# The two-layer loop written out on every engine, with constants where a register counted the layer

## What is computed

```python
for layer in range(DEPTH):                      # DEPTH = 2
    shift, scale, gate = ada_modulation(c, w_mod_mix[layer], b_mod_mix[layer])
    h = normalize(x) * (1.0 + scale) + shift
    mix = token_mixer(h, ...)                   # stick-breaking attention, pooling mixer,
                                                # sliding-window attention, sigmoid gates, w_out
    x = layer_norm(DEEPNORM_ALPHA * x + (1.0 + gate) * mix, ln_mix_g[layer], ln_mix_b[layer])
    shift, scale, gate = ada_modulation(c, w_mod_ffn[layer], b_mod_ffn[layer])
    h = normalize(x) * (1.0 + scale) + shift
    if layer % 2 == 0:
        ff = swiglu(h, ffn_w1[0], ffn_w3[0], ffn_w2[0])          # D_FF = 2816
    else:
        ff = moe_swiglu(h, w_router[0], b_router[0], exp_w1[0], exp_w3[0], exp_w2[0])
                                                # 8 experts of width 3584, the best 2 for each token
    x = layer_norm(DEEPNORM_ALPHA * x + (1.0 + gate) * ff, ln_ffn_g[layer], ln_ffn_b[layer])
```

## Time and profile before

| | before |
|---|---|
| median of 3 runs | 1914.64 us (1914.64, 1905.44, 1916.42) |
| span of the profiled execution | 1919.3 us |
| PE busy | 1731.4 us (90%) |
| DVE busy | 1421.4 us (74%) |
| ACT busy | 1042.3 us (54%) |
| POOL busy | 25.5 us (1%) |
| DMA | 503.98 MB, mean 263 GB/s |

### The profile page before, as it was taken

The page is one execution under the profiler, slowest core; times in us unless marked ns, Lnnn a source line. Parts: engine busy times, 40 slices in busy tenths (PEclk is TensorE's granted clock), DMA queues, the critical chain, the costliest instruction groups (busy, mean ns, idle before and its releaser), DMA issues.

```text
span 1919.3 us, 22270 instructions
## 1 busy us (share of the span) xinstructions
PE 1731.4 (90%) x7882; PEld 1390.2 (72%) x7883; DVE 1421.4 (74%) x1201; ACT 1042.3 (54%) x817; POOL 25.5 (1%) x31
## 2 busy tenths in 40 slices
PE   1899979996999949989979989999899899999995
PEld 0787758885877727868868868887687687787784
DVE  7776877757676776877868866656588688787787
ACT  1465434433555326757747745554577576675773
POOL 0100000000000000000000000000000000000000
PEclk9998989998999969999999999999999999999998
DMA  9874458754665436987978965666599699799892
GB/s 367 309 271 144 154 186 315 275 182 171 249 214 179 145 115 240 357 327 274 362 288 306 363 253 197 219 219 219 180 354 380 236 362 363 278 359 344 300 362 83
DMA packets 210686, 503.98 MB, mean 263 GB/s; under 512 B 9137, under 2 KB 13409, under 8 KB 210481
## 3 DMA queue, kind: packets, MB, share of 16 engines
q1 hardware_dynamic: 208770, 496.15, 72.3%
q0 software_dynamic: 1712, 5.43, 0.9%
HBM read 500.50 MB, written 1.05 MB: 261 GB/s over the span
## 4 chain that ended last, share of the span: by engine, by line
PE 79%; DVE 10%; issue 8%; ACT 2%; DMA 1%; DVEq 0%; ACTq 0%; SPq 0%
PE ps L1241 22%; PE ps L1243 22%; PE ps L1242 22%; DVE w_lo L772 2%; PE ps L1247 2%; PE ps L1248 2%; PE ps L1644 2%; PE ps L1530 2%; PE ps L1686 1%; DVE mod_acc L797 1%; ACT w_hi L457 1%; DVE stats L817 1%; PE ps L1365 1%; DVE gates L966 1%; PE ps L1366 1%
## 5 line engine op out<-in xcount | busy, mean ns | idle before, releaser
L772 DVE TENSOR_TENSOR w_lo<-w_raw,w_hi 128x2048 fp32r<-128x2048 f32 x423 | 966.4, 2291 | 381.7 <-ACT w_hi L457 381.1
L457 ACT CAST w_hi<-w_raw 128x2048 fp32r<-128x2048 f32 x423 | 806.5, 1910 | 352.0 <-PE ps L1243 282.7
L1241 PE MATMUL ps<-w_hi,actT_hi 128*128 128x512 f32 (+1 forms) x1536 | 613.8, 400 | 60.0 <-issue 40.2
L1243 PE MATMUL ps<-w_hi,actT_lo 128*128 128x512 f32 (+1 forms) x1536 | 600.0, 391 | 0.0
L1242 PE MATMUL ps<-w_lo,actT_hi 128*128 128x512 f32 (+1 forms) x1536 | 599.4, 390 | 0.0
L1241 PEld LDWEIGHTS ps<-w_hi,actT_hi 128*128 128x128 f32 x1536 | 294.3, 192 | 132.3 <-issue 60.9
L1243 PEld LDWEIGHTS ps<-w_hi,actT_lo 128*128 128x128 f32 x1536 | 293.3, 191 | 61.6
L1242 PEld LDWEIGHTS ps<-w_lo,actT_hi 128*128 128x128 f32 x1536 | 294.8, 192 | 57.5 <-issue 1.0
L1241 PE MATMUL ps<-w_hi,gT_hi 128*128 128x512 f32 x536 | 213.1, 398 | 16.3 <-DVE gT_lo L1058 14.1
L1243 PE MATMUL ps<-w_hi,gT_lo 128*128 128x512 f32 x536 | 213.6, 398 | 0.0
L1242 PE MATMUL ps<-w_lo,gT_hi 128*128 128x512 f32 x536 | 213.2, 398 | 0.0
(11 more groups left out here) (225 smaller groups left out, 1070.3 us busy)
## 6 DMA issues: line engine op xcount, KB each, us to landing
w_raw<-in_exp_w_dram SPq DMA_DIRECT2D x336, 1024.0 KB, 7.0
w_raw<-in_ffn_w_dram SPq DMA_DIRECT2D x33, 1024.0 KB, 5.2
w_raw<-in_w_mod_mix_dram SPq DMA_DIRECT2D x24, 1024.0 KB, 8.1
w_raw<-in_w_mod_ffn_dram SPq DMA_DIRECT2D x24, 1024.0 KB, 5.3
w_raw<-in_w_gate_dram SPq DMA_DIRECT2D x24, 1024.0 KB, 5.7
w_raw<-in_w_in_dram SPq DMA_DIRECT2D x14, 1024.0 KB, 7.3
w_raw<-in_w_out_dram SPq DMA_DIRECT2D x8, 1024.0 KB, 5.1
w_raw<-in_w_branch_c_dram SPq DMA_DIRECT2D x4, 1024.0 KB, 5.0
```

The source lines that it names most:

```text
L457: nc.scalar.copy(w_hi[:, j % SPLIT, :], w_raw[:, i % RING, :]).then_inc(split_hi, 1)
L772: TTn(w_lo[:, j % SPLIT, :], w_raw[:, i % RING, :], w_hi[:, j % SPLIT, :].bitcast(F32), ALU.subtract).then_inc(piece_used, 1)
L1241: MM(to, hi, w_h, start=first, stop=False)
L1243: return MM(to, lo, w_h, start=False, stop=last)
```

## The change

On all five engines the loop `Fori(0, DEPTH)` becomes Python's `for layer in range(DEPTH)`, so the code of the token mixer is laid down twice, once for each layer, and `layer` is a number when the program is built. `If(layer < 1)` / `Else` becomes Python's `if` / `else`, so the dense half stands behind the first mixer and the expert half behind the second, with no branch between. Waits that counted with a register have a constant. No arithmetic, no buffer, no transfer and no order of work on any engine is altered, and the experts' loop with its own branches stays.

```diff
--- before.py
+++ after.py
@@ -385,11 +385,11 @@
             stream(MOD0, 0, None, mod_layer=("mix", 0))
-            with sp.Fori(0, DEPTH) as layer:
+            for layer in range(DEPTH):
                 stream(MIX, layer * LAYER_PIECES + MOD0.n, layer, mod_layer=("ffn", layer), gap=layer * (RING // 2))
-                with sp.If(layer < 1):
+                if layer < 1:
                     stream(DENSE, MOD0.n + MIX.n, 0, mod_layer=("mix", 1), gap=RING // 2)
-                with sp.Else():
+                else:
                     moe0 = MOD0.n + LAYER_PIECES + MIX.n
                     sp.wait_ge(piece_used, moe0 + RING)
@@ -417,7 +417,7 @@
             gp.dma_start(cst[:, C_PAST:], consts[:, C_PAST:]).then_inc(tables_loaded, 16)
-            with gp.Fori(0, DEPTH) as layer:
+            for layer in range(DEPTH):
                 gp.wait_ge(gate1_ready, layer * 2 + 1)
                 gp.dma_start(sinks[:, :], I["sinks"][bass.ds(layer, 1), :].rearrange("a h -> (a h)").partition_broadcast(P)).then_inc(small_loaded, 16)
@@ -432,12 +432,12 @@
                         I["ln_mix_b"][bass.ds(layer, 1), :].rearrange("a d -> (a d)"))
-                with gp.If(layer < 1):
+                if layer < 1:
                     gp.wait_ge(gate_sent, 2)
                     fresh_acc(I["b_mod_mix"][1:2, :], 2)
                     gp.wait_ge(x_ready, 2)
                     ln_rows(I["ln_ffn_g"][0], I["ln_ffn_b"][0])
-                with gp.Else():
+                else:
                     gp.wait_ge(x_ready, 4)
                     nc.gpsimd.memset(yacc[:, :, :], 0.0).then_inc(yacc_zero, 1)
@@ -518,7 +518,7 @@
 
-            with act.Fori(0, DEPTH) as layer:
+            for layer in range(DEPTH):
                 sbase = layer * LAYER_SPLITS
                 chain = Chain(act, act_mix, layer * ACT_MIX_STEPS)
@@ -670,11 +670,11 @@
 
-                with act.If(layer < 1):
+                if layer < 1:
                     stream(DENSE, [MOD0.landed[s] + MIX.landed[s] for s in range(RING)], MIX.n_split,
                            panel_events(DENSE, DENSE_PANELS, MIX.n_split, 0, 2))
                     norms(2, 6, 4, 0, lambda i: round_piece(MIX, i, [layer_loads[s] + MOD0.landed[s] for s in range(RING)], LAYER_SPLITS))
-                with act.Else():
+                else:
                     act.wait_ge(rt_loaded, 32)
                     A(w_rt_hi[:, :, :], w_rt[:, :, :], ACT.Copy).then_inc(rt_hi, 1)
@@ -910,7 +910,7 @@
 
-            with dve.Fori(0, DEPTH) as layer:
+            for layer in range(DEPTH):
                 sbase = layer * LAYER_SPLITS
                 chain = Chain(dve, dve_mix, layer * DVE_MIX_STEPS)
@@ -1087,7 +1087,7 @@
 
-                with dve.If(layer < 1):
+                if layer < 1:
                     chain = Chain(dve, dve_ffn, 0)
                     stream(DENSE, [MOD0.landed[s] + MIX.landed[s] for s in range(RING)], MIX.n_split,
@@ -1095,7 +1095,7 @@
                     assert chain.n == DVE_DENSE_STEPS, chain.n
-                with dve.Else():
+                else:
                     chain = Chain(dve, dve_ffn, DVE_DENSE_STEPS)
                     step = chain.step
@@ -1290,7 +1290,7 @@
             open_sublayer(0, 4, 0, MOD0.n)
-            with pe.Fori(0, DEPTH) as layer:
+            for layer in range(DEPTH):
                 pbase = layer * LAYER_PIECES + MOD0.n
 
@@ -1605,11 +1605,11 @@
 
-                with pe.If(layer < 1):
+                if layer < 1:
                     swiglu(DENSE, DENSE_PANELS, MOD0.n + MIX.n, 0, 2)
                     pe.wait_ge(piece_used, LAYER_PIECES + MOD0.n + RING)
                     open_sublayer(2, 4, 0)
-                with pe.Else():
+                else:
                     second_tile(3, 4)
                     open_tile(3, 0, 1)
```

## The result

The changed kernel takes 1928.78 us (median of 6 runs, 1926.59 to 1933.76), the kernel before 1914.67 us (median of 6, 1905.44 to 1918.67). The ratio is 1.0088, with a 95% interval from 1.0065 to 1.0112. The forecast was 1906 us, with a range up to 1919 us: it was wrong in its sign and in its range.

A forecast was written before the change was run, and what follows sets the result against it. It took TensorE (PE), busy 90% of the span, as the bound, with its uncovered far jumps as the gain: 6.7 + 2.0 + 0 + 0 = 8.7 us off the 1914.64 us median, giving 1906 us, range 1896 to 1919 us.

The forecast's parts named there:

- Part 1: At the layer loop's closing, PE's bare jump back goes and the third weight piece starts earlier: 6.7 us gained.
- Part 2: Where the second layer branches to the experts, VectorE's jump goes and line 1102 follows line 858 directly: 2.0 us gained.
- Part 3: Register additions for the token mixer's waits run in the sequencers ahead of the engines: priced at 0, other end 1 us.
- The covered jumps: Jumps of ScalarE, GpSimd and SyncE in the layers, and PE's own to the experts, lie behind other work: 0.
- Part 4: In the experts' loop the code moves but keeps its size: priced at 0, with both ends put into rivals.
- Rival 2: Experts' code lies worse; two cheap boundaries turn dear, or each round pays one more fetch: 1914.7 us, chance 0.18.
- Rival 1: Experts' code lies better and PE keeps the body from the first rounds on: 1893 us, chance 0.12.
- Rival 3: Jumps are not what PE waited for, or the mixer gives the gain back: about 1914 us, chance 0.10.

The follow-up runs named there:

- e1: The change on SyncE, GpSimd, ScalarE and VectorE alone, PE keeping the two-layer loop of the kernel before; 1919.01 us, ratio 0.9983.
- e2: The change on PE alone, the other four engines keeping loop and branches of the kernel before; 1929.66 us, ratio 1.0068.
- e3: The changed kernel with 314 satisfied waits (157 instructions) at PE's start, giving the experts' code its old offset within a packet; 1907.85 us, ratio 0.9945.
- e4: The kernel before with 198 satisfied waits (99 instructions) at PE's start, giving the experts' code the changed kernel's packet offset; 1937.06 us, ratio 1.0102.
- shift by 40: The changed kernel with 80 satisfied waits (40 instructions) at the start of PE's program; 1920.61 us, ratio 1.0028.
- shift 64: The changed kernel with 128 satisfied waits (64 instructions) at the start of PE's program; 1907.65 us, ratio 0.9961.
- e12: The changed kernel unaltered, run beside the shifted ones on the same chip; 1927.07 us, ratio 1.0051 to the kernel before.
- e14: e13 with 254 satisfied waits (127 instructions) added, so that a round touches eight packets; 1897.61 us, ratio 0.9904.
- shifts 64 and 157: The changed kernel with satisfied waits at PE's start that move its code by 64 instructions (1907.65 us) or 157 (1907.85 us).
- e13: The changed kernel with PE's gathering for an expert's second block moved to the head of the two-block bodies; 1917.24 us, ratio 1.0003.
- shifts 0, 40, 206 and 256: The changed kernel unshifted (1927.07 us), or with PE's code moved by satisfied waits by 40 (1920.61 us), 206 (1932.82 us) or 256 instructions (1928.07 us).
- e15: e14 with the experts' loops of ScalarE and VectorE written out, PE keeping its loop; 1881.22 us, ratio 0.9818.

## Why the prediction was wrong, and where it was right

**Part 1, the back edge: right.** 6.4 us measured in the two profiles for 6.7, with the wait that takes its place (line 772) and the clock as forecast. The prediction took 487.34 us from the chain as the third piece's start, where the timeline has 487.10 us; that is most of the difference. Its own sign for this part, a second token mixer shorter by 6 to 7 us, came true: from line 858 at the closing to line 858 ahead of the experts it took 227.1 us and takes 220.5 us.

**Part 2, the branch to the experts: right.** 2.14 us for 2.0, and e1 has it alone.

**Part 3, the register instructions: not refuted at 0.** The first branch on the count comes 10.0 us earlier. 6.4 and 2.1 us of it are named, 0.8 us lie ahead of the loop's closing, and some 0.6 us in the rest of the mixer and behind the routing. The 0.8 us can't be put down to anything: over the profiled executions line 858 at the closing starts anywhere from 468.1 to 472.9 us.

**The covered jumps: right.** e2 shows two of DVE's in a row, 8.98 us in all, with PE at work.

With the experts' code at its old offset the sum of these parts stands in the measured time too: e3 is 8.8 us under the kernel before, forecast 8.7. That it agrees to 0.1 us is luck; the interval of its ratio runs from 5 to 16 us.

**Part 4, the experts: this step failed.** It says "The edit changes the place of head and body, not their size, so I price this part at 0". The place cost 19.0 us in the two profiled executions, and by the medians some 23 us (14.1 us slower where 8.7 us faster was forecast); e4, which only moves the code of the kernel before, lost 20.4 us. The step had no measurement behind its 0: it did not count how many packets a round needs, though its own rows showed them being fetched. The rounds fit a PE that keeps eight packets and a one-block round that touches nine, and two things then depended on the offset within a packet:
- With a border among the instructions skipped just ahead of the loop's head, line 1659's branch takes 5.8 us in place of 4.4 us, mostly with two packets side by side. The likely reading, which is argued and not shown, is that PE asks for the packet behind the border, which it never uses, together with the head's. The shift by 40 gets 6.5 us back.
- In the kernel before, the late rounds kept their code. The two boundaries that cost 2.93 and 2.73 us then cost 8.12 and 9.19 us now. Rounds 7 and 8, from one branch at line 1698 to the next, took 5.2 and 4.0 us longer; the other six together 9.7 us, of which the packed round has 3.9 us. The step from shift 40 to shift 64 is worth 13.0 us.

**The rivals.** Rival 2 had the sign, and named both mechanisms: two cheap boundaries that turn, or one more fetch in each round. It gave them as alternatives and priced one, 8.8 us; both happened. With both of its prices, 8.8 + 8 x 1.1 = 17.6 us, it would have said 1905.9 + 17.6 = 1923.5 us, over the range's end of 1919 us. Its argument against ("both kinds occur with one placing, so the place alone doesn't set it") held only for the placing at hand. Side by side on one chip, the kernel before took 1904 to 1931 us in 24 runs and the changed kernel 1924 to 1929 us in 8. That fits a number of cheap rounds that differs from one execution to the next at the one offset and is none at the other; it isn't shown for the kernel before, of which there is one profile; the changed kernel's two (the second is e12's) have no cheap late round. Rival 1, a better placing, named 1893 us, and no shift of the changed kernel came near it: the best took 1907.65 us. To come within 5 us of it took a shorter body as well (e14, 1897.61 us). Rival 3 fell with parts 1 and 2.

The wide spread of the kernel before was visible in its three runs (1905.44 to 1916.42 us), and the two kinds of boundary in its profile. Together they said that the experts stood near an edge, and a range that ended 4 us above one price of rival 2 was too narrow for it.

**What the stops rest on.** The Trainium skill, page "Runtime: NRT & Kernel Launch", section Instruction fetch mechanics, gives PE 128 KiB for instructions in blocks of 16 KiB, which makes eight. The runs agree in the main: with eight packets in a round five rounds of e14 fetched none, with nine every round up to the next branch into the body fetched at least two and most fetched eight or nine. The same section also says "there's no instruction cache that benefits from spatial locality" and speaks of only two lines. Here the trace differs: in e14 PE went through whole rounds of eight packets, jumping between two places some 17 packets apart (4,356 instructions in the built program), without a single packet on q8.

**Left open.** Why nine packets sometimes settle into rounds with two fetches (shifts 64 and 157, e13, the kernel before) and not at shifts 0, 40, 206 and 256 isn't settled, and neither is why eight did so in e15. Nor is why the head's branch stayed at 5.5 us in e13, with one packet and no border in the skipped instructions. That the dear branch of the changed kernel comes from two packets at once rests on the queue's rows and on the shifts, with e13 against it; a run with the second packet alone removed wasn't made.

## What to carry to other kernels

An edit that adds or removes instructions ahead of a loop moves that loop's code against the instruction packets. If the loop has far jumps on the bounding engine, price the loop's boundaries at both of their kinds and let the range hold both; a wide spread over a few runs says that they can flip. Count the packets that a round touches, with the one fetched ahead at each place. Here it was one more than the eight that the engine seems to keep; a shift by 64 instructions was worth 19.4 us, and bringing the round into eight packets another 10 us (1897.61 for 1907.65, in two groups), where the unrolled outer loop brought 8.8 us (e3). And once the bounding engine's jumps are short, look at those of the engines that feed it.

## What the runs showed of the hardware

- A far jump on PE took 0.2 us where no packet came for it. A long branch took 3.3 to 6.0 us with one packet (median 4.0 us) and 4.2 to 7.4 us with two at once (median 5.6 us).
- PE held eight packets of 16 KB (some 250 instructions each) over whole rounds of e14 and fetched none. A round of nine fetched eight or nine of them mostly, and never fewer than two. The same loop of eight fetched two a round at the end of e15.
- Shifting the same program by 40 instructions changed its time by 6.5 us, by 64 by 19.4 us (1927.07 - 1907.65), by 256 by 1 us (1928.07 for 1927.07), which is noise.
- The stops also cost clock: behind the stop of 5.13 us PE's granted clock was 0.50 for 4.2 us, and 1.00 at the same place without the stop. The mean is 0.949 in the changed kernel's profiled execution and 0.963 in e15's.
